# Three plain feed-forward pairs before Strassen's, the split ahead of x's normalisation, and all sums on the vector engine

## What is computed

```python
D_MODEL = 1024
SEQ = 512
D_FF = 2816
def rmsnorm(x, g):
    xf = x.astype(jnp.float32)
    y = xf * lax.rsqrt(jnp.mean(xf * xf, axis=-1, keepdims=True) + RMS_EPS)
    return (y * g.astype(jnp.float32)).astype(x.dtype)
def swiglu(x, wg, wu, wd):
    return (jax.nn.silu(x @ wg) * (x @ wu)) @ wd
...
        x = x + 0.5 * swiglu(rmsnorm(x, ffn1_norm[l]), ffn1_wg[l], ffn1_wu[l], ffn1_wd[l])
```

## Time and profile before

| | |
|---|---|
| time, median of 3 runs (lowest, highest) | 2085.74 us (2083.86, 2087.57) |
| the profiled execution: its own time | 2087.14 us |
| its span, first to last instruction | 2085.3 us |
| mean granted TensorE clock | 0.967 of full speed |
| PE matmuls, share of the span with one in flight | 92% |
| DVE / ACT / POOL busy | 72% / 45% / 38% |

### The profile page before, as it was taken

One profiled execution on the slowest core, in us unless ns is written; L12 is line 12 of the kernel. 1 busy time (PEld: TensorE's weight loads), 2 busy tenths in 40 slices (PEclk: granted clock), 3 DMA queues, 4 the chain that ended last, 5 costly groups with the idle time before them and its releaser, 6 DMA issues.

```text
span 2085.3 us, 32543 instructions
## 1 busy us (share of the span) xinstructions
PE 1928.6 (92%) x11480; PEld 1693.1 (81%) x11480; DVE 1493.0 (72%) x1734; ACT 940.5 (45%) x1608; POOL 799.3 (38%) x522
## 2 busy tenths in 40 slices
PE   6999999997989899999998999999949998999997
PEld 4899978785868789997877999788736877999885
DVE  7799933567778689983367999436887567999434
ACT  4455522436346445452244454324547544454322
POOL 4666500213122466650036666002247436666001
PEclk9999999999989999999999999999979999999998
DMA  4122332222211213233222232322210022232321
GB/s 144 61 101 101 104 113 87 93 83 50 81 41 41 82 60 102 99 107 115 90 72 81 87 108 89 120 101 89 81 61 21 24 79 68 94 104 97 121 101 41
DMA packets 36170, 176.94 MB, mean 85 GB/s; under 512 B 12688, under 2 KB 13072, under 8 KB 15488
## 3 DMA queue, kind: packets, MB, share of 16 engines
q1 hardware_dynamic: 33696, 172.55, 24.3%
q10 hardware_dynamic: 2240, 2.98, 0.4%
q0 software_dynamic: 160, 0.43, 0.1%
HBM read 173.85 MB, written 2.10 MB: 84 GB/s over the span
## 4 chain that ended last, share of the span: by engine, by line
PE 61%; DVE 20%; issue 10%; ACT 5%; POOL 2%; DMA 1%; DVEq 1%; ACTq 0%; POOLq 0%; SPq 0%
PE ps L294 20%; PE ps L296 19%; PE ps L295 19%; DVE wl L507 7%; DVE tml L611 2%; DVE tg L552 1%; DVE wl L264 1%; ACT wh L496 1%; DVE a L739 1%; DVE a L552 1%; DMA raw<-in_units 1%; DVE xgl L342 1%; ACT wh L260 1%; DVE rB L391 1%; POOL sg L776 1%
## 5 line engine op out<-in xcount | busy, mean ns | idle before, releaser
L294 PE MATMUL ps<-xgh,wh 128*128 128x256 f32 (+1 forms) x1504 | 511.6, 340 | 59.1 <-DVE wl L264 26.1
L295 PE MATMUL ps<-xgl,wh 128*128 128x256 f32 (+1 forms) x1504 | 502.2, 334 | 0.0
L296 PE MATMUL ps<-xgh,wl 128*128 128x256 f32 (+1 forms) x1504 | 501.8, 334 | 0.0
L294 PE MATMUL ps<-tmh,wh 128*128 128x256 f32 (+1 forms) x1472 | 457.0, 310 | 10.9 <-ACT mc L531 5.5
L264 DVE TENSOR_TENSOR wl<-raw,wh 128x2048 fp32r<-128x2048 f32 (+1 forms) x85 | 199.0, 2341 | 361.7 <-ACT wh L260 361.6
L296 PE MATMUL ps<-tmh,wl 128*128 128x256 f32 (+1 forms) x1472 | 450.3, 306 | 0.0
L295 PE MATMUL ps<-tml,wh 128*128 128x256 f32 (+1 forms) x1472 | 450.3, 306 | 0.0
L294 PEld LDWEIGHTS ps<-xgh,wh 128*128 128x128 f32 x1504 | 292.5, 194 | 94.7 <-DVE wl L264 28.9
L525 POOL TENSOR_TENSOR ws<-raw 128x512 f32<-128x512 f32 x144 | 250.4, 1739 | 267.7 <-DVE wl L507 190.8
L260 ACT ACTIVATE wh<-raw 128x2048 fp32r<-128x2048 f32 (+1 forms) x85 | 161.2, 1896 | 386.9 <-PE ps L296 385.7
L507 DVE TENSOR_TENSOR wl<-raw,wh 128x512 fp32r<-128x512 f32 x216 | 324.3, 1527 | 0.0
(11 more groups left out here) (267 smaller groups left out, 2898.1 us busy)
## 6 DMA issues: line engine op xcount, KB each, us to landing
raw<-in_units SPq DMA_DIRECT2D x161, 1024.0 KB, 4.8
x<-in_xT ACTq DMA_DIRECT2D x4, 512.0 KB, 7.5
outT<-x SPq DMA_DIRECT2D x8, 256.0 KB, 2.1
relb<-in_rpb SPq DMA_DIRECT2D x64, 24.0 KB, 2.2
cosA<-in_rope_a ACTq DMA_DIRECT2D x1, 256.0 KB, 2.5
sinA<-in_rope_a ACTq DMA_DIRECT2D x1, 256.0 KB, 2.9
cosD<-in_rope_d POOLq DMA_DIRECT2D x1, 192.0 KB, 3.0
sinD<-in_rope_d POOLq DMA_DIRECT2D x1, 192.0 KB, 2.9
```

The source lines that it names most:

```text
L294: nc.tensor.matmul(dst, lh, rh, start=first, stop=False, skip_group_check=onto)
L295: nc.tensor.matmul(dst, lh, rl, start=False, stop=False, skip_group_check=onto)
L296: return nc.tensor.matmul(dst, ll, rh, start=False, stop=last, skip_group_check=onto)
```

## The change

- NS = 3: three plain pairs and eight of Strassen's in each FFN.
- `split_lo` of pair 1's first unit comes ahead of `xn`; the eight `xn` instructions are cut into two groups of four with work of the pairs between them.
- POOL's `right_pool` and `left_sums_pool` are gone. Their work is done by DVE: `right_sums` in plain pair 1, `left_sum`, one sum at a time, in the steps j = 0 to 3 (the pair's second unit) and 8 to 11 (the next pair's first unit) of `prods_dve`. POOL keeps the factor `rB` on `sg`.
- The split of the differences of x (`sums_hi`, `sums_lo`) moves into plain pair 1, one plain pair before the last.
- At the end of the last Strassen pair, ACT's and DVE's splits for the down projection's first unit and first activations move into the steps j = 8 to 11.
- The semaphore by which a unit's slot is free again (`w_half`) rises at step 10 in place of 9.

```diff
-NS = 2
+NS = 3
...
-            if j in (9, 13):
-                eng.wait_ge(w_half, 2 * (B + 2 * NS + 2 * r) + (2 if j == 9 else 4))
+            if j in (10, 13):
+                eng.wait_ge(w_half, 2 * (B + 2 * NS + 2 * r) + (2 if j == 10 else 4))
...
-        def left_sums_pool(pool, f, B, r, x_):
+        def left_sum(dve, f, B, r, x_, i):
...
+            if i == 0:
+                dve.wait_ge(raw_in[c % 2], 16 * r + 16 * (c // 2 + 1))
+            if x_:
+                dve.wait_ge(s_lo, left_count(f, r, (4, 2, 3, 5)[i]) - (3 if first and i in (1, 2) else 0))
+            elif not first:
+                dve.wait_ge(s_lo, left_count(f, r - 1, (10, 8, 11, 12)[i]))
+            if i in (1, 3):
+                dve.wait_ge(s_sum, (4 + 8 * RP) * f + 4 + 8 * r + 4 * x_ + i)
+            nc.vector.tensor_tensor(ws[:, i, :], u, v, op).then_inc(s_sum, 1)
...
-        def prods_act(act, f, B, r, r_next):
+        def prods_act(act, f, B, r, r_next, c_down=None):
             for j in range(N_STEP):
                 if j in (0, 2, 4, 6, 8, 10):
                     copy_act(act, f, B, r, j)
+                if j == 10 and r_next is None:
+                    split_hi(act, c_down)
...
+                    if r_next is None:
+                        a_hi_act(act, f, 0)
...
+                if j < 4:
+                    left_sum(dve, f, B, r, 1, j)
+                if 8 <= j < 12 and r_next is not None:
+                    left_sum(dve, f, B, r_next, 0, j - 8)
                 if j + 5 < N_STEP:
                     left_lo(dve, f, B, r, j + 5)
...
+                if j == 9 and r_next is None:
+                    a_lo_dve(dve, f, 0)
...
         def ffn_dve(dve, f, B, n, last):
...
+            split_lo(dve, B + 1)
+            norm_dve(dve, n)
+            dve.wait_ge(rstd, n + 1)
             for p in range(NS):
-                split_lo(dve, B + 2 * p + 1)
...
                 if p < NS - 1:
                     split_lo(dve, B + 2 * p + 2)
-                else:
+                if p == 0:
+                    for k in range(4):
+                        normed(k)
+                if p == 1:
+                    right_sums(dve, f)
                     for t in range(4):
                         sums_lo(dve, f, t)
+                if p == NS - 1:
+                    for i in range(4):
+                        left_sum(dve, f, B, 0, 0, i)
                     for j in range(4):
                         left_lo(dve, f, B, 0, j)
                     right_lo(dve, f, 0)
...
+                if p < NS - 1:
+                    split_lo(dve, B + 2 * p + 3)
+                if p == 0:
+                    for k in range(4, KD):
+                        normed(k)
...
-            prods_dve(dve, f, B, RP - 1, None, c)
-            a_lo_dve(dve, f, 0)
```

More of the change, by code:

```diff
@@ L474, in prod_pe @@
                            k == 0 and a in (A11, A12, S3, S4), k == 3, a in (S2, S1, A22))
-            mm.then_inc(*((w_half, 2) if j in (9, 13) else (s_prod, 1)))
+            mm.then_inc(*((w_half, 2) if j in (10, 13) else (s_prod, 1)))
         def prods_pe(pe, f, B, r):
@@ L508, in left_lo @@
             ins.then_inc(w_lo if a == A22 else s_lo, 1)
-        def left_sums_pool(pool, f, B, r, x_):
+        def left_sum(dve, f, B, r, x_, i):
             first = isinstance(r, int) and r == 0
             c = B + 2 * NS + x_
[L514 to L525, removed]
+            q = [raw[:, c % 2, n * 512:(n + 1) * 512] for n in range(4)]
+            u, v, op = ((q[2], q[3], ALU.add), (ws[:, S1, :], q[0], ALU.subtract),
+                        (q[0], q[2], ALU.subtract), (q[1], ws[:, S2, :], ALU.subtract))[i]
+            if i == 0:
[7 more added lines that the diff above has]
+            nc.vector.tensor_tensor(ws[:, i, :], u, v, op).then_inc(s_sum, 1)
         def copy_act(act, f, B, r, j):
@@ L594, in right_pool @@
                 if i < 2:
-                    pool.wait_ge(xn_done, 8 * f + 4 * (i + 1))
+                    dve.wait_ge(xn_done, 8 * f + 4 * (i + 1))
                 else:
-                    pool.wait_ge(s_sum, done + 2 * i - 3)
-                nc.gpsimd.tensor_tensor(tm32[:, dst], u, v, ALU.subtract).then_inc(s_sum, 1)
+                    dve.wait_ge(s_sum, done + 2 * i - 3)
+                nc.vector.tensor_tensor(tm32[:, dst], u, v, ALU.subtract).then_inc(s_sum, 1)
         def right_part(i):
@@ L701, in ffn_act @@
                     split_hi(act, B + 2 * p + 2)
-            for t in range(4):
-                sums_hi(act, f, t)
+                if p == 1:
+                    for t in range(4):
+                        sums_hi(act, f, t)
             for j in range(4):
@@ L772, in ffn_pool @@
             pool.wait_ge(rstd, n + 1)
-            for p in range(NS):
-                for m in range(2):
-                    pool.wait_ge(silu_done, 22 * f + 2 * p + m + 1)
-                    nc.gpsimd.tensor_tensor(sg[:, m, :], sg[:, m, :], rB[:, :], ALU.mult).then_inc(s2_done, 1)
-                if p == 0:
-                    right_pool(pool, f)
-            for x_ in range(2):
-                left_sums_pool(pool, f, B, 0, x_)
-            with pool.Fori(1, RP) as r:
-                for x_ in range(2):
-                    left_sums_pool(pool, f, B, r, x_)
+            for m in range(2 * NS):
+                pool.wait_ge(silu_done, 22 * f + m + 1)
+                nc.gpsimd.tensor_tensor(sg[:, m % 2, :], sg[:, m % 2, :], rB[:, :], ALU.mult).then_inc(s2_done, 1)
             finish_pool(pool, n + 1)
```

14 lines of the change are left out of this document (6 added, 8 removed).

## The result

The changed kernel takes 1994.27 us, the median of 3 runs (1991.63 to 1995.74). Against the kernel before that is a ratio of 0.956, 95% interval 0.9538 to 0.9581. The forecast was 1993, with a range of 1984 to 2012.

The account below looks back on a forecast made before the run. PE was taken as the bound, with some 26 us per FFN of waits or slow matmuls to win. Terms of -85.9 and -7.5 gave -93.4: 1992.3 against 2085.74, stated as 1993, range 1984 to 2012.

Parts of the forecast that it names:

- the stretches: Second plain unit's first matmul to the down projection's first, four FFNs: 958.66 to 872.8 us, -85.9.
- the rest: Outside those windows: slow matmuls behind the wait before the down projection go, -7.5 us over four FFNs.
- A plain pair for a Strassen pair: In each FFN, 21.76 us of matmuls replace 20.16: +1.60 us.
- The split ahead of xn: Before plain pair 1: split done at about 717.0, the 6.24 us wait and its slow matmuls go, slack 0.3 to 0.6.
- x's low parts: Before the second Strassen step: DVE's two products, then the low part, leave a 1.2 us wait; bounds nothing and 4.35.
- The estimate for the stage: Reciprocal to first Strassen step: 49.5 us of DVE work fit within PE's 54.4 us of matmuls.
- Sums within the pairs: Strassen loop: DVE busy 17.8 to 18.5 us a trip, under PE's 20.16, so the 0.84 per trip goes.
- rivals about VectorE (1 and 2): Strassen loop: waits stay, up to +27 us, 2020, chance 0.13; or DVE becomes the bound, +139, 2132, chance 0.04.
- The end of the pairs: Before the down projection: of 3.65 us idle 0.4 stay, 0.5 with the slower start.
- Rival 4: Clock falls at the remaining 1.2 us wait before the second Strassen step: 1.65 us per FFN, 2000, chance 0.06.

Follow-up runs that it names:

- an edit made by the wrong one: Changed kernel with the low part of x's lower half made on VectorE ahead of its two last plain products: 1997.8 us, ratio 0.9581.
- The two experiments with POOL: Changed kernel with sums of weights back on POOL: 2016.3 us; changed kernel with eight unneeded POOL additions in each Strassen pair: 2186.4 us.
- halves: Changed kernel with x's lower half and the down projection's first unit split in two pieces, ScalarE's other high parts behind its first copy: 1993.8 us, ratio 0.9559.

## Why the prediction was right

The sum came out in its terms: the stretches by -86.1 us for -85.9, the rest by -6.7 for -7.5. Undone one at a time, the four parts cost 24.8 (sums of weights), 20.0 (third plain pair), 20.9 (split ahead of xn) and 13.5 us (end of the pairs) in the stretches, 79.2 of the 86.1 together. Two parts were not tried alone: x's differences on VectorE one plain pair earlier, and the semaphore that rises at step 10.

**A plain pair for a Strassen pair, +1.60.** Right to the hundredth (four plain pairs: +1.60 again).

**The split ahead of xn.** The wait of 6.24 us is gone with a slack of 0.42 us, where 0.3 to 0.6 was forecast. Done alone it would have moved most of the wait to the next place; only with the third plain pair is it worth its full price. The prediction counted both, but did not say that the first hangs on the second. Its "about 717.0" for the end of the split rests on ScalarE's high part, and that is what the trace shows ahead of the split (2.51 us of idle time).

**x's low parts.** The size was right (1.14 for 1.2) and the step behind it wrong: "when the last plain matmul ends, DVE has two products (1.2) and then the low part of x's lower half (1.17) before step 1 can start". What is behind the wait is ScalarE's high part, about 1.0 us, which can only start when the last plain matmul has read the old content, and then the low part, 1.2. The two chains are of nearly the same length, so that the number held by luck; an edit made by the wrong one gained nothing and cost 3.7 us. The estimate for the stage, 49.5 us of VectorE work, was too high: its busy time is 43.07. `xn` takes 0.68 us each without POOL and not 1.2, which makes 4.1 us. And the sum has five splits of a unit where only four lie behind the reciprocal: that of pair 0's second unit starts at 680.00, and the reciprocal at 686.81. That makes 2.2.

**Sums within the pairs.** A trip takes 20.16 us and VectorE is busy for 17.78 of it (17.8 to 18.5 forecast). Both rivals about VectorE (1 and 2) rested on the question whether POOL lengthens its operations. The two experiments with POOL show that it does, and that it is worth the 0.84 per trip. The prediction's 17.8 us came out to the hundredth, with the sums at the 0.60 that it had no row of VectorE for. The room left over, though, is less than the idle time says.

**The end of the pairs.** 0.44 in place of 0.5, released by VectorE's split of the unit.

**The clock.** Rival 4 did not happen: behind the 0.98 us wait 66 matmuls of 256 tokens lie in 8 us at a clock of 1.00. FFN 0 starts at the lower clock as before, 28 matmuls in 8 us, and its stretch is 1.28 us longer than the others (1.65 forecast). The -7.5 outside of the stretches came out as -6.7, but with the scatter there (1116.7 to 1123.0 us) this is no confirmation of the term; what confirms it is the window behind the down projection's start, 35 matmuls where 28 were.

## What to carry to other kernels

Work on a second engine isn't free because that engine is idle: here, with POOL busy for 13 us of a trip, VectorE was busy for 19.73 us, and for 17.78 when it made the sums itself. The sign is a mean duration that differs between groups of one shape and operation (1571 and 887 ns with POOL, 686 for both without it). Where a stage is short of an engine's time, reordering moves a wait and doesn't remove it; add the engine's work over the stage first, then order it. And an engine's room is not its idle time: look at which wait of another engine's queue its result releases, and what useful work is queued behind that.

## What the runs showed of the hardware

- A POOL addition that reads SBUF delays VectorE's operations with two SBUF inputs though their data have nothing to do with each other: 1.52 us in place of 0.68, one for one. A combination with an input in PSUM (L554, at 892.40 in the window above, while POOL adds) took 0.41 us, as it does without POOL.
- Waits of TensorE of 0.98 us left its granted clock at 1.00. Behind 3.65 and 6.41 us the mean over 8 us was 0.82 and 0.80, some of it at the lower of the two levels, 1.2 GHz, and the rest at 2.4.
- The same piece of a mixer was at a granted clock of 0.80 in one execution and 1.00 in another, 2.1 us apart, with nothing changed in it. The start of FFN 0 too is one or the other: 0.79 over 8 us in the changed kernel, 1.00 in the execution with halves, whose first stretch is 217.7 us and not 219:

```profile
31.31:39.31 8.00, 8.00 (x35) 6.62 (x36) 5.46 (x4) 3.04 (x3) 2.56 (x2) 1.00 0.37 133
```
